# Layer 0 of a two-layer diffusion backbone block: gates and Fourier input in one-pass products, a new order of vector work, a ring table, and a tail by halves

## What is computed

```
p   = a @ w_in                      # columns: fourier 512 | ssm 512 | gate a 1024 | gate b 1024
y_a = fft2(p_fourier).real @ w_four
y_s = gelu(s5_scan(p_ssm))          # diagonal complex state space, both directions
y_b = (y_s @ w_glu_a) * sigmoid(y_s @ w_glu_b)
out = (sigmoid(p_ga) * y_a + sigmoid(p_gb) * y_b) @ w_out
h  += g1 * out ;  h += g2 * channel_mixer(norm(h))
# channel mixer: dense SwiGLU in layer 0, top-2-of-8 expert SwiGLU in layer 1
```

## Time and profile before

| | us |
|---|---|
| median of 3 runs | 2035.4 |
| lowest, highest run | 2034.87, 2527.94 |
| the profiled execution's own time | 2034.36 |
| its span (first to last instruction) | 2032.6 |
| PE busy in the span | 1982.9 |
| DVE busy | 1535.1 |
| ACT busy | 962.4 |
| mean granted TensorE clock | 0.996 of full |

### The profile page before, as it was taken

One profiled execution on the slowest core, in us unless ns is written; L12 is line 12 of the kernel. 1 busy time (PEld: TensorE's weight loads), 2 busy tenths in 40 slices (PEclk: granted clock), 3 DMA queues, 4 the chain that ended last, 5 costly groups with the idle time before them and its releaser, 6 DMA issues.

```text
span 2032.6 us, 24902 instructions
## 1 busy us (share of the span) xinstructions
PE 1982.9 (98%) x10214; PEld 1556.2 (77%) x10214; DVE 1535.1 (76%) x2009; ACT 962.4 (47%) x885; POOL 0.2 (0%) x4
## 2 busy tenths in 40 slices
PE   6999999999999999999999999999999999999998
PEld 3545774577788778889878888888888888888886
DVE  7788537777755774480588898888989898898986
ACT  2312212322212222411267766777767777677775
POOL 0000000000000000000000000000000000000000
PEclk9999999999999999999999999999999999999999
DMA  9345675324533443585279999899998999899994
GB/s 401 103 164 172 162 258 204 117 83 181 186 146 150 179 163 135 162 212 187 84 296 378 365 366 372 331 368 359 373 353 339 373 355 375 337 366 369 355 368 173
DMA packets 83841, 529.29 MB, mean 260 GB/s; under 512 B 23056, under 2 KB 49552, under 8 KB 52752
## 3 DMA queue, kind: packets, MB, share of 16 engines
q1 hardware_dynamic: 62976, 508.65, 67.5%
q10 hardware_dynamic: 20752, 19.05, 2.7%
HBM read 509.39 MB, written 18.28 MB: 260 GB/s over the span
## 4 chain that ended last, share of the span: by engine, by line
PE 89%; DVE 7%; ACT 1%; DMA 1%; issue 1%; ACTq 1%; SPq 0%; DVEq 0%
PE ps L2490 15%; PE ps L2475 15%; PE ps L2476 15%; PE ps L1948 10%; PE ps L1957 6%; PE ps L1964 6%; PE ps L1961 6%; PE ps L2285 1%; PE ps L2124 1%; PE ps L2419 1%; DMA ring<-in_w_mod 1%; PE ps L2230 1%; DVE H L1596 1%; DVE sc L1594 1%; PE ps L2293 1%
## 5 line engine op out<-in xcount | busy, mean ns | idle before, releaser
L1771 DVE TENSOR_TENSOR WL<-mring,WH 128x2048 fp32r<-128x2048 f32 x336 | 755.1, 2288 | 102.3 <-ACT WH L1085 102.1
L1085 ACT ACTIVATE WH<-mring 128x2048 fp32r<-128x2048 f32 x336 | 626.2, 1913 | 144.1 <-PE ps L2490 107.4
L2475 PE MATMUL ps<-WH,XGh 128*128 128x512 f32 x896 | 353.8, 395 | 0.2 <-issue 0.2
L2476 PE MATMUL ps<-WH,XGl 128*128 128x512 f32 x896 | 349.4, 390 | 0.0
L2490 PE MATMUL ps<-WL,XGh 128*128 128x512 f32 x896 | 221.6, 389 | 0.0
L2490 PEld LDWEIGHTS ps<-WL,XGh 128*128 128x128 f32 x896 | 168.2, 188 | 34.9
L2475 PEld LDWEIGHTS ps<-WH,XGh 128*128 128x128 f32 x896 | 168.3, 188 | 33.9 <-issue 0.3
L2476 PEld LDWEIGHTS ps<-WH,XGl 128*128 128x128 f32 x896 | 168.4, 188 | 33.4
L2475 PE MATMUL ps<-WH,hTh 128*128 128x512 f32 x448 | 175.8, 392 | 0.0
L2476 PE MATMUL ps<-WH,hTl 128*128 128x512 f32 x448 | 174.5, 390 | 0.0
L869 ACT ACTIVATE FWH<-ring 128x4096 fp32r<-128x4096 f32 (+2 forms) x21 | 67.9, 3233 | 217.8 <-DMA ring<-in_ffn_gu 126.9
(11 more groups left out here) (370 smaller groups left out, 2498.2 us busy)
## 6 DMA issues: line engine op xcount, KB each, us to landing
mring<-in_moe_gate SPq DMA_DIRECT2D x56, 2048.0 KB, 9.4
mring<-in_moe_up SPq DMA_DIRECT2D x56, 2048.0 KB, 9.6
mring<-in_moe_down SPq DMA_DIRECT2D x56, 2048.0 KB, 9.1
ring<-in_w_mod SPq DMA_DIRECT2D x23, 2048.0 KB, 8.1
ring<-in_w_in SPq DMA_DIRECT2D x11, 2048.0 KB, 11.5
ring<-in_ffn_gu SPq DMA_DIRECT2D x11, 2048.0 KB, 8.0
ring<-cks SPq DMA_DIRECT2D x4, 2048.0 KB, 11.2
ring<-in_w_out SPq DMA_DIRECT2D x4, 2048.0 KB, 8.3
```

The source lines that it names most:

```text
L1085: nc.scalar.activation(WH[buf][:, o], mring[t % MRING][:, o], ACT.Copy).then_inc(high_done, 1)
L1771: V.tensor_tensor(WL[buf][:, o], mring[t % MRING][:, o], WH[buf][:, o].bitcast(F32), ALU.subtract).then_inc(low_done, 1)
L2475: mm(out_, ah, WH[buf][:, o:o + 512], start=(first and q == 0), stop=False)
L2476: mm(out_, al, WH[buf][:, o:o + 512], start=False, stop=False)
```

## The change

In layer 0:

- `gate_a(k)` for k = 2 to 7 and the four Fourier input blocks become split products. One list `BLOCKS` holds ga 2 to 7 (indices 0 to 5), f 0 to 3 (6 to 9) and gb 0 to 7 (10 to 17, `GATES` = 10); `block_high(i)`, `block_low(i)` and `split_block(i)` take the place of `gate_high`, `gate_low` and `split_gate`. ga 0 and 1 stay plain.
- The input high parts are made right after the shift, the low parts right after ga 1. The eight copies of `E` go to ScalarE (`state_inputs_out`).
- `out_powers(0, k)` and `lag_rows` stand ahead of the scan, with `block_low(2 + k)` between them; `lags(0, n)` run between gate a and Fourier blocks.
- The scan is five loops (2, 3, 1, 1, 1 iterations), with `lag_rows(0, 1)` and four `block_low` between them.
- `in_powers(1, n)` for n = 2 to 5 gets buffers of its own in `aT`; `turn(1, 0)` follows gb 6, `mod_sums(9)` and `turn(1, 1)` follow `Y`, and `turn(1, 2)` to `turn(1, 7)` lie between the `ya` products.
- The ring stream has a new order, and slots of layer 0 come from a table.

In the tail, the last tile is computed by output halves (`last_outputs`), and `yeh` and `yel` of the first half start when it is done.

```diff
-        stream += mods(6) + [("w_in", 0, 0)] + mods(7) + [("w_in", 0, 4)] + mods(8) + [("w_in", 0, 5)] + mods(9)
-        stream += [("ck", 0, 0), ("toep", 0, 0), ("ck", 0, 1), ("w_four", 0, 0)] + mods(10)
-        stream += [("ys", 0, 0), ("ys", 0, 1), ("w_glu_b", 0, 0)] + mods(11) + [("w_glu_a", 0, 0)]
+        stream += [("w_in", 0, 0)] + mods(6) + [("w_in", 0, 4)] + mods(7) + [("w_in", 0, 5)] + mods(8)
+        stream += [("ck", 0, 0), ("toep", 0, 0), ("ck", 0, 1), ("w_four", 0, 0)] + mods(9)
+        stream += [("ys", 0, 0), ("ys", 0, 1)] + mods(10) + [("w_glu_b", 0, 0)] + mods(11) + [("w_glu_a", 0, 0)]
...
+        SLOT_OF = {("w_in", 0, 0): 2, ("mod", 0, 6): 1, ("w_in", 0, 4): 1, ("mod", 0, 7): 0, ("w_in", 0, 5): 0,
+                   ("mod", 0, 8): 2, ("ck", 0, 0): 2, ("ck", 0, 1): 1, ("w_four", 0, 0): 0, ("mod", 0, 9): 2,
...
+        BLOCKS = [("ga", 0, m) for m in range(2, 8)] + [("f", 0, m) for m in range(4)] + [("gb", 0, m) for m in range(8)]
+        BLOCK_HIGH = [GA0] + [GAs[i % 4] for i in range(9)] + [GH0, GH1, GH2, GH1, GH4, GH5, GH4, GH5]
...
                 shift(l, 0)
+                if l == 0:
+                    inputs_high()
...
+                    for m in range(4):
+                        for d in range(2):
+                            state_inputs_out(m, d)
+                            if (m, d) == (0, 0):
+                                block_high(0)
+                            if m == 2:
+                                block_high(1 + d)
+                    block_high(3)
+                    block_high(4)
                     for i in range(ITS):
                         masked(0, i)
...
+                    for k in range(2, 8):
+                        evac(("ga", l, k), G[:, k, t0:NT], ACT.Sigmoid, n)
+                        if k > 2:
+                            block_high(k + 2)
+                            store_reads(0, k - 3)
...
                     evac(("gb", l, m), G2[:, m, t0:NT], ACT.Sigmoid, n)
                     if l == 0 and m < 6:
-                        gate_high(m + 2)
+                        block_high(GATES + m + 2)
...
+                if l == 0:
+                    inputs_low()
+                    block_low(0)
+                    block_low(1)
+                    _, done, _, at, _ = place(("E", 0, 3, 1))
+                    dve.wait_ge(done, at + 1)
+                    for k in range(ITS):
+                        out_powers(0, k)
+                        if k == 6:
+                            lag_rows(0, 0)
+                        block_low(2 + k)
...
+                if l == 0:
+                    scan(0, 2)
+                    lag_rows(0, 1)
+                    scan(2, 5)
+                    block_low(GATES)
+                    block_low(GATES + 1)
+                    scan(5, 6)
+                    block_low(GATES + 2)
+                    scan(6, 7)
+                    block_low(GATES + 3)
+                    scan(7, 8)
...
+                    block_low(GATES + 4)
                     mod_columns(1)
                     powers(1)
                     tables(1)
+                    in_powers(1, 0)
+                    for m in range(5, 8):
+                        block_low(GATES + m)
+                    for k in range(1, 6):
                         in_powers(1, k)
...
                     for k in range(2, 8):
-                        gate_a(k)
+                        split_block(BLOCKS.index(("ga", 0, k)))
                         if k == 5:
                             mod_sums(6)
+                        if k > 2:
+                            lags(0, k - 3)
                     fourier_in()
...
+                    for m in range(8):
+                        split_block(GATES + m)
+                        if m == 6:
+                            turn(1, 0)
...
+            def last_outputs(outs, wh, wl, high):
+
+                pe.wait_ge(high_done, high + 2)
+                for h, (out_, pairs, _, _) in enumerate(outs):
+                    for (ah, al), o in pairs:
+                        mm(out_, ah, wh[:, o:o + 512], start=False, stop=False)
+                        mm(out_, al, wh[:, o:o + 512], start=False, stop=False)
+                    pe.wait_ge(low_done, high + 2)
+                    for q, ((ah, _), o) in enumerate(pairs):
+                        last = mm(out_, ah, wl[:, o:o + 512], start=False, stop=(q == len(pairs) - 1))
+                    last.then_inc(first_half if h == 0 else tile_done, 1)
...
             for j in range(4):
+                pe.wait_ge(ye_low, 2 * NE - 1 + j // 2)
```

More of the change, by code:

```diff
@@ L238, in program @@
         side([("lag", 0, mh) for mh in range(2)], (4,))
-        side([("turn", 1, n, r) for n in range(3) for r in range(2)])
+        side([("turn", 1, 0, r) for r in range(2)])
         side([("Y", 0, mh, c) for mh in range(2) for c in range(2)])
-        side([("turn", 1, n, r) for n in range(3, ITS) for r in range(2)])
+        side([("turn", 1, n, r) for n in range(1, ITS) for r in range(2)])
         side([("lag", 1, mh) for mh in range(2)])
@@ L420, in program @@
         out0_high.close()
[L421 to L427, removed]
+        blocks_first = ExitStack()
+        GA0 = sb(blocks_first, "GA0", [P, D], F32R)
+        sb(blocks_first, "left0", [P, SLOT - D])
+        GAs = [sb(blocks_first, f"GA{i + 1}", [P, D], F32R) for i in range(4)]
+        blocks_first.close()
+        blocks_second = ExitStack()
+        sb(blocks_second, "left1", [P, 512])
+        GH0 = sb(blocks_second, "GH0", [P, D], F32R)
+        sb(blocks_second, "left2", [P, 512])
+        GH2 = sb(blocks_second, "GH2", [P, D], F32R)
+        GH1 = sb(blocks_second, "GH1", [P, D], F32R)
+        blocks_second.close()
         GR = sb(mix, "GR", [P, 2 * SLOT])
@@ L1010, in _ @@
                 if l == 0:
[L1011 removed]
+                    for i in range(1, ITS):
                         turned(1, i)
[L1013 removed]
                 for m in range(8):
@@ L1112, in pair @@
                     x = e + NE * pas
+                    if pas:
+                        act.wait_ge(tile_done, x * TILES)
+                        for h in range(2):
+                            outputs_high(h, 1 - par)
                     for t, (kind, c) in enumerate(moe_order):
+                        if (kind, c) == ("down", 6) and at_end(pas, i, par):
+                            continue
                         act.wait_ge(tile_done, x * TILES + t + 1)
@@ L1468, in inputs_low @@
             def inputs_low():
-                _, done, _, at, _ = place(("f", 0, 3))
+                _, done, _, at, _ = place(("ga", 0, 1))
                 dve.wait_ge(done, at + 1)
@@ L1600, in _ @@
                 if l == 0:
-                    for k in range(ITS):
-                        out_powers(0, k)
-                        if k == 6:
-                            lag_rows(0, 0)
-                    inputs_low()
-                    gate_low(0)
-                    gate_low(1)
-                    lag_rows(0, 1)
-                    gate_low(2)
+                    block_low(GATES + 4)
                     mod_columns(1)
-                    gate_low(3)
                     powers(1)
-                    gate_low(4)
@@ L1800, in pair @@
                     head = pas == 0 and (i, par) == (0, 0)
+                    if pas:
+                        for h in range(2):
+                            dve.wait_ge(ye_ready, x * 2 + h - 1)
+                            outputs_low(h, 1 - par)
                     for t, (kind, c) in enumerate(moe_order):
@@ L1848, in _ @@
                 pairs_of(dve, 1, lambda i: pair(1, i))
+                dve.wait_ge(ye_ready, 4 * NE)
+            for h in range(2):
+                dve.wait_ge(ye_ready, 2 * NE - 1 + h)
+                outputs_low(h, 1)
             for m in range(KD):
@@ L2175, in fourier_in @@
                 def fourier_in():
-                    wf = slot(("w_in", l, 0))[:].rearrange("p (k c) -> p k c", k=KD)
                     for m in range(4):
-                        product(("f", l, m), [(wf[:, k, P * m:P * m + P], aT[:, k, t0:NT]) for k in range(KD)], n_)
-                        if l == 0 and m == 1:
+                        split_block(BLOCKS.index(("f", 0, m)))
+                        if m == 1:
                             mod_sums(7)
-                        if l == 0 and m >= 2:
-                            lags(0, m - 2)
+                        if m < 3:
+                            lags(0, 5 + m)
                 def first_transform():
@@ L2297, in _ @@
                 if l == 0:
-                    turn(1, 3)
+                    mod_sums(9)
+                    turn(1, 1)
                 w = slot(("w_four", l, 0))[:].rearrange("p (k c) -> p k c", k=MB)
```

275 lines of the change are left out of this document (133 added, 142 removed).

## The result

| | before | after |
|---|---|---|
| median of the runs, us | 2035.6 (4 runs) | 2017.6 (4 runs, 2015.6 to 2018.6) |
| ratio of the runs, 95% interval | | 0.9912 (0.9892 to 0.9931) |
| profiled execution, us | 2034.4 | 2017.8 |
| its span, us | 2032.6 | 2016.0 |

The change takes 18 us, 0.9%, off the median and 16.6 off the profiled execution. The prediction was 2019.3 us (2008 to 2027). One of the four runs of the kernel before took 2527.94 us; it is a slow run, and the ratio leaves it out.

The account below looks back on a forecast made before the run. TensorE, busy 1982.9 of 2032.6 us, was taken as the bound. 2034.4 profiled less 13.3 (front, after new waits) and 2.8 (tail) gave 2018.3; the median, 1.0 above, 2019.3, range 2008 to 2027.

Parts of the forecast that it names:

- forecast A: The main forecast: TensorE stalls in gate b on VectorE's chain; 2019.3 us, own range 2016 to 2023, chance 0.55.
- The passes: Ten gate a and Fourier blocks go from 6.92 to 5.59 us each: 13.3 us less on TensorE.
- TensorE's layout: TensorE's schedule from ga 2 at 97.3 us: lag 7 ends at 156.0, gb 0 starts at 186.3.
- VectorE's layout: VectorE's schedule: powers and early lows done at 138.7, scan iterations 7.6 each, gb 4's low part ends at 212.3.
- Rival C: VectorE's chain slips further through a late store before `out_powers(0, 7)`, loop entries and `mod` 9: 2024.3 us, chance 0.25.
- the wait of 1.8 in gb 4: In gate b TensorE wants gb 4's low part at 210.5, VectorE has it at 212.3: 1.8 us idle.
- The wait in gb 5: TensorE waits 7.0 us for VectorE's low part, ready at 224.9; `Y` then starts at 243.4, 17.0 earlier.
- Behind `Y`: `mod_sums(9)` (1.9) and two turns (1.8) now follow `Y`, so 13.3 of the 17.0 us gained remain.
- The moved loads: The ring's reordered loads cost nothing, hidden by TensorE's blocks; the thinnest, `mod` 9, would cost up to 2 us.
- The tail: Last tile by halves: the first half's operations end before the tile does, adds start at 2017.8, 2.8 us less.
- D: Rival: each of four new scan loop entries waits 8.1 us for instructions, giving 2048 us; chance 0.05.

Follow-up runs that it names:

- The early low part: Changed kernel with VectorE making the low parts of gb 5 to 7 between powers(1), tables(1) and in_powers(1, 0), not behind all three: 2010.8 us.
- the tail alone: Kernel before with only the last tile computed by halves, nothing else of the change: 2034.2 us, ratio 0.9983.

## Why the prediction was right

The time came out 1.7 us under the point, and forecast A's picture was the right one. That the number came so close was in part luck. The profiled execution was predicted at 2018.3 and took 2017.8, but the front gave 15.1 and not 13.3, and 1.4 of that went again in the experts, where nothing was changed and executions differ by as much. The rest of the 1.7 is the median of the runs, taken as 1.0 above the profiled execution; it was 0.2 below. Step by step:

**The passes**: right. 13.3 predicted; with plain blocks put back, the time rose by 12.1 and `Y` came 12.7 later. The rule of the Trainium skill on four passes (FP8 and Floating Point Precision, TensorE Precision Notes), by which the gain was estimated at 17.3, was rightly left aside: of a split block's three passes each takes 5.59 / 3 = 1.86 us, but the plain block 6.92, less than four of them (7.45).

**TensorE's layout**: lag 7 ended at 157.4, predicted 156.0; gb 0 started at 186.69, predicted 186.3. A block between two lags takes 5.79 (151.08 to 156.87), not 5.59, which the layout left out; the stretch from f 3 to gb 0 gave most of it back.

**VectorE's layout**: two terms were mis-sized, in opposite directions. Rival C's mechanism, a store that lands late, was real, but it struck `out_powers(0, 4)`, not (0, 7): the store took 10.8 us from its issue, and I had allowed 4.0 to 7.4. Its 3.1 us fell into slack: the powers were done at 141.7 and not 138.7, and the wait for lag 7 was 0.8 and not 2.1. And the scan's single iterations took 6.3, not 7.6. gb 2's low part waited 3.5 (predicted 3.6) and started at 194.16 (predicted 193.5); with two short iterations behind it, gb 4's low ended at 210.6 and not at 212.3. So the wait of 1.8 in gb 4, a step of the forecast, did not occur: TensorE asked for that low at 211.0.

**The wait in gb 5**: 6.6, predicted 7.0; its end at 223.4, predicted 224.9; from there to `Y` 18.6, predicted 16.8 + 1.7. The early low part showed that it is a matter of order in VectorE's list alone. At `Y` the gain was 18.4, predicted 17.0. The 1.4 come from VectorE's list, which sets this time: gb 4's low part ended 1.7 earlier than laid out, by the two short iterations. The missing wait in gb 4 added nothing, since TensorE only came to the stop in gb 5 that much earlier. Behind `Y` 3.7 go off, as predicted: `glub` starts at 301.53, 14.7 earlier.

**The moved loads** were priced at nothing, and cost nothing: behind the first loads no wait of TensorE for the ring is in the trace.

**The tail**: 2.9, predicted 2.8, but by another margin than told. The first half was to be done before the tile ends. A table load of ScalarE, 1.28 us at 1999.67, which the prediction missed, stood in its way (in the kernel before it came behind `yeh`, at 2018.94): `yeh` began at 2001.08 though its bank had been full since 1999.9. VectorE's half ended at 2002.53, 0.05 before the tile. In the run of the tail alone it ended 0.13 behind the tile (2020.31 for 2020.18), and the adds still started 1.42 behind it: in both traces they start as VectorE ends its second half.

**D**, the loops: refuted. No gap at a loop's start is above 0.6, with five loops or eight. One sum on D was wrong: 2076 us would have taken not nearly three times its price but under twice, (2076 - 2019.3 + 3.6) / 32.4 = 1.9. The Trainium skill's rule on fetches (Runtime: NRT & Kernel Launch, Instruction fetch mechanics) shows nothing here; whether these loops lie within the pages it speaks of can't be told from the trace.

What the prediction did not look for: TensorE's wait for the mixed features near 350 us. It was 2.3 before and 2.9 after, from ScalarE's queue. In the trace of before the same store takes 6.14 us to issue at the same place, so the 3.1 us were probably there to be had in it too; that wasn't run.

```profile
354.16 6.14 ACTq L816 DMA_DIRECT2D gds<-Gs  x1
```

Open: why the issue of that store takes 7.00 us on ScalarE's queue and 0.59 when it comes later. That more transfers are in the queue at the earlier place is likely, but it wasn't tried alone.

## What to carry to other kernels

When two engines run side by side within a few us, list the slack of the second at each point where it waits for the first: the sum (7.4 us here) bounded what a speed-up of the first was worth. Count the waits that reach the first engine through a third one, too: two of the three here went through ScalarE's high part and through a store. Where a new order creates a wait, look whether the item waited for is ready to be made earlier in the other engine's list; three lines moved gave 7.5 us, more than half of what ten cheaper blocks gave. Before a reader of a bank is moved back, name the next writer of that bank; and look what stands behind a long DMA issue in an engine's own queue.

## What the hardware showed beside

- A step of the scan takes 0.90 us in a loop that turns and 0.79 in a loop of one iteration. In the timeline of the former the third operation of a step starts 0.24 behind the second (151.65 to 151.89), in the latter 0.13 (152.13 to 152.26). The source of the step is the same (`Fori(lo, hi)`); the waits' values and the addresses in `H` are written with the loop's counter. Why the step is slower in a loop that turns wasn't isolated.
- The store of 512 KB in front of `out_powers(0, 4)` took 10.8 us. It was issued at 109.03, a load of 2 MB at 109.02 and the next store at 115.40. Issued at 103.56, 5.8 after the load before that one and 5.6 ahead of the next, it took 3.9. That the load begun with it made it slow is likely, but wasn't tried apart from the other changes of place. The median of the four stores out of these buffers is 8.4 (in the kernel before 5.5).
- 6.6 us of idle time brought the granted clock to 0.50 and cost 1.5 to 2.8 us, not the same in each execution; 2.9 us of idle time at `glua` left the next eight matmuls at 3.70, the same as those before.
